# Expert outputs through rows in HBM: scatter by indirect DMA and a token-major final norm

## The reference

```python
def rms_norm(x, g):
    y = x * lax.rsqrt(jnp.mean(x * x, axis=-1, keepdims=True) + EPS)
    return y * g

def moe(h, router, w1, w3, w2):
    logits = h @ router
    top_v, top_i = lax.top_k(logits, TOP_K)
    gates = jax.nn.softmax(top_v, axis=-1)
    dense_gate = jnp.sum(jax.nn.one_hot(top_i, N_EXPERTS) * gates[..., None], axis=-2)
    out = jnp.zeros_like(h)
    for e in range(N_EXPERTS):
        out = out + dense_gate[..., e:e + 1] * swiglu(h, w1[e], w3[e], w2[e])
    return out

x = x + moe(h, ...)
y = rms_norm(x, W['norm_final'])
```

## Time and profile before

| | |
|---|---|
| time, median of 3 runs | 1873.12 us (1873.08 to 1874.67) |
| profiled execution, its own time | 1880.72 us |
| its span, first to last instruction | 1878.6 us |
| PE busy | 1783.1 us, 95% of the span |
| DVE, ACT, POOL busy | 1136.1, 945.4, 81.2 us |
| HBM read and written | 384.78 and 6.08 MB |
| granted TensorE clock, mean | 0.96 of full speed |

### The profile page before, as it was taken

How to read it: one execution, slowest core, us unless ns; L and a number is a source line. 1 busy time by engine, 2 the same in 40 slices (tenths; PEclk the granted TensorE clock), 3 DMA queues, 4 the chain that set the end, 5 groups by cost and what they waited for, 6 DMA issues and landing times.

```text
span 1878.6 us, 32676 instructions
## 1 busy us (share of the span) xinstructions
PE 1783.1 (95%) x13577; PEld 1579.2 (84%) x13577; DVE 1136.1 (60%) x1294; ACT 945.4 (50%) x1073; POOL 81.2 (4%) x136
## 2 busy tenths in 40 slices
PE   7999999999999999999879999999999999999995
PEld 6778878899998788878779889898989989898893
DVE  5166215355543255315348878787887878787884
ACT  2344424353433144333336757676666767665672
POOL 3000110020001000020000000000000000000000
PEclk9999889899999999979879999999999999999998
DMA  8124343155457223435178979898997989899860
GB/s 198 51 91 136 126 123 119 50 173 166 151 154 180 72 86 126 134 102 164 50 264 278 362 262 366 273 365 289 330 366 260 361 274 367 288 332 344 279 214 26
DMA packets 350355, 392.22 MB, mean 209 GB/s; under 512 B 24652, under 2 KB 324840, under 8 KB 350264
## 3 DMA queue, kind: packets, MB, share of 16 engines
q1 hardware_dynamic: 345328, 381.05, 62.1%
q0 software_dynamic: 4640, 9.76, 1.5%
q10 hardware_dynamic: 296, 0.07, 0.0%
HBM read 384.78 MB, written 6.08 MB: 208 GB/s over the span
## 4 chain that ended last, share of the span: by engine, by line
PE 89%; ACT 4%; DVE 4%; issue 1%; DMA 1%; POOL 0%; DVEq 0%; ACTq 0%; SPq 0%
PE ps L607 87%; ACT ring L1106 1%; DVE w_lo L1892 1%; PE ps L1030 1%; ACT w_hi L1106 1%; ACT L1106 1%; ACT kvw_hi L1106 1%; DVE dw_lo L1457 1%; DVE ring L1748 1%; ACT low L1106 0%; DMA ring<-in_ffd_w_dram 0%; PE ps L1080 0%; DMA ring<-in_x_sample_dram 0%; PE ps L905 0%; DVE att L1755 0%
## 5 line engine op out<-in xcount | busy, mean ns | idle before, releaser
L1892 DVE TENSOR_TENSOR w_lo<-ring,w_hi 128x2048 fp32r<-128x2048 f32 x264 | 603.5, 2291 | 86.7 <-ACT w_hi L1106 79.3
L1106 ACT ACTIVATE w_hi<-ring 128x2048 fp32r<-128x2048 f32 x264 | 504.9, 1913 | 139.1 <-PE ps L607 138.4
L607 PE MATMUL ps<-w_hi,hg_hi 128*96 128x256 f32 x1408 | 398.3, 283 | 2.1 <-DVE hg_lo L1869 2.1
L607 PE MATMUL ps<-w_hi,hg_lo 128*96 128x256 f32 x1408 | 394.4, 280 | 0.0
L607 PE MATMUL ps<-w_lo,hg_hi 128*96 128x256 f32 x1408 | 393.8, 280 | 0.0
L607 PEld LDWEIGHTS ps<-w_hi,hg_hi 128*96 128x96 f32 x1408 | 228.1, 162 | 8.7 <-issue 2.3
L607 PEld LDWEIGHTS ps<-w_lo,hg_hi 128*96 128x96 f32 x1408 | 227.4, 162 | 5.7
L607 PEld LDWEIGHTS ps<-w_hi,hg_lo 128*96 128x96 f32 x1408 | 228.6, 162 | 0.0
L1457 DVE TENSOR_TENSOR dw_lo<-ring,dw_hi 128x2048 fp32r<-128x2048 f32 (+1 forms) x54 | 113.1, 2094 | 113.8 <-ACT dw_hi L1106 113.8
L1106 ACT ACTIVATE low<-ps 96x256 f32<-96x256 f32 (+6 forms) x170 | 66.2, 396 | 190.1 <-PE ps L607 179.4
L1106 ACT ACTIVATE dw_hi<-ring 128x2048 fp32r<-128x2048 f32 (+1 forms) x54 | 94.6, 1752 | 101.5 <-PE ps L607 62.1
(11 more groups left out here) (277 smaller groups left out, 2790.6 us busy)
## 6 DMA issues: line engine op xcount, KB each, us to landing
ring<-in_moe_w_dram SPq DMA_DIRECT2D x264, 1024.0 KB, 5.8
ring<-in_ffd_w_dram SPq DMA_DIRECT2D x22, 1024.0 KB, 5.3
ring<-in_ffd_w_dram SPq DMA_DIRECT2D x16, 704.0 KB, 4.6
ring<-in_w_in_dram SPq DMA_DIRECT2D x14, 768.0 KB, 4.5
ring<-in_w_in_dram SPq DMA_DIRECT2D x8, 1024.0 KB, 5.4
ring<-in_xa_wk_dram SPq DMA_DIRECT2D x8, 1024.0 KB, 5.2
ring<-in_xa_wv_dram SPq DMA_DIRECT2D x8, 1024.0 KB, 5.2
ring<-in_xa_wq_dram SPq DMA_DIRECT2D x8, 1024.0 KB, 5.1
```

Of the source, the lines that this page charges most:

```text
L607: return nc.tensor.matmul(out, lhsT, rhs, start=first, stop=last)
L1106: return nc.scalar.activation(out, in_, func, **kw)
L1892: V.tensor_tensor(view(w_lo, off, SLOT), view(ring, moe_slot(u) * SLOT, SLOT), view(w_hi, off, SLOT).bitcast(F32), ALU.subtract).then_inc( ...
```

## The change

The result of an expert no longer goes to `xT` by products on PE. An internal tensor `moe_rows` in HBM has 2 x 288 rows of 1024 numbers, one row for each token's first and second expert, and 96 spare rows. After an expert, DVE copies its unscaled result to `y_sb` (`copy_y`), and POOL writes the 96 rows of it by an indirect DMA to the rows whose numbers stand in `row_at`. POOL waits for that DMA and then signals `y_free`; DVE waits for `y_free` before it writes the next row numbers. The row numbers come from three products in `gather` (`sel` times `id_col`), in the place of the three that gave the gate weights. ACT fills the 576 rows with zeros once, in layer 0, by a DMA from a tile of zeros.

Between the router and the first expert, PE transposes `xT` to token-major form (`turn_x`, 24 transposes) and ACT copies it to `acc`. `small` is transposed, copied and stored there as well. In the last expert, POOL reads the 2 x 288 rows back, and DVE adds them to `acc` with the gate weight of each token as a scalar, three instructions after step 4 and three after step 8 (`add_back`). The last expert's own result is split in high and low part, multiplied by `selT` (12 products of 512 columns) and added to `acc` with its gate weights. The final norm runs token-major: a sum of squares along the row and the root on ACT, one scaling per tile on DVE, and three stores on SP. SP also loads the gains of the final norm, spread over 128 partitions, before it goes on with the ring.

The core of the diff; new semaphores and memory places are left out:

```diff
-            def scatter(n):
-                pe.wait_ge(y_scaled, n + 1)
-                for d in range(KD):
-                    if d >= 4:
-                        pe.wait_ge(scat_added, n * KD + d - 3)
-                    mm(ps[:, 4 + d % 4, 0:T], y_sb[0:C, P * d:P * d + P], selT[0:C, :], True, True).then_inc(scat_ready, 1)
...
                 up(0)
-                scatter(it)
                 up(1)
-                pe.wait_ge(scat_added, it * KD + KD)
-                for t in range(3):
-                    nc.tensor.transpose(ps[0:C, 6, P * t:P * t + P], sel[:, t, :], ident[:, :])
-                for t in range(3):
-                    last = mm(ps[0:C, 6, 384:385], sel[:, t, :], gcol[:, t:t + 1], t == 0, t == 2)
+                if last_one:
+                    for t in range(3):
+                        last = nc.tensor.transpose(ps[0:C, 6, P * t:P * t + P], sel[:, t, :], ident[:, :])
...
+            with pool.Fori(0, more * NE + NE) as it:
+                pool.wait_ge(y_scaled, it + 1)
+                pool.sem_inc(y_taken, 1)
+                pool.indirect_dma_start(rows_y[:, :], bass.IndirectOffsetOnAxis(ap=row_at[0:C, 0:1], axis=0),
+                                        y_sb[0:C, :], None).then_inc(y_put, 16)
+                pool.wait_ge(y_put, it * 16 + 16)
+                pool.sem_inc(y_free, 1)
...
+            gather(1)
+            turn_x(2)
+            b = open_bank("small")
+            close_bank(nc.tensor.transpose(ps[0:32, b, 0:P], small[:, :], ident[:, :]))
+            pe.wait_ge(act_emptied, emptied("xt", 5))
+            pe.wait_ge(small_ready, 1)
...
-            V.memset(ps[0:C, 2:4, :], 0.0)
-            V.memset(gs[0:C, :], 0.0)
-            link(V.memset(selT[0:C, :], 0.0))
...
-                scale_y(it)
+                copy_y(it)
                 weight_lo(it, 2)
-                add_y(it)
                 weight_lo(it, 3)
...
+                    dve.wait_ge(y_free, it + 1)
+                    V.tensor_scalar(row_at[0:C, :], ps[0:C, 6, 0:1], spare_row[0:C, 0:1], None, ALU.add)
...
+                    if last_one and s in (4, 8):
+                        add_back(s // 4 - 1)
...
+            for half in range(2):
+                f(y_hi[0:C, 512 * half:512 * half + 512], ps[0:C, 2 + half, :], ACT.Copy).then_inc(y_hi_done, 1)
+            for t, (t0, rows) in enumerate(TILES):
+                act.wait_ge(acc_ready, t + 1)
+                f(y_sb[0:rows, :], acc[t], ACT.Square, accum_out=msq_y[0:rows, t:t + 1]).then_inc(rs_step, 1)
...
```

More of the change, by code:

```diff
@@ L216, in layer_program @@
         sel = view(low, 6976, 3, C)
-        selT = view(low, 7264, T)
+        tok_no = view(low, 7552, 3, NE)
+        row_no = view(low, 7576, 3, NE)
+        id_col = view(low, 7600, 3)
+        spare_row = view(low, 7604, 1)
+        row_at = view(low, 7606, 1).bitcast(U32)
+        msq_y = view(low, 7608, 3)
+        rs_y = view(low, 7612, 3)
+        ids = view(low, 7616, 3, (MAXR + 1) * NE)
         lgt = view(low, 7936, 3, NE)
@@ L986, in _, with turn_x @@
             close_bank(last)
+            def turn_x(t):
+                t0, rows = TILES[t]
+                for g in range(2):
+                    b_ = open_bank("xt")
+                    for j in range(4):
+                        last_ = nc.tensor.transpose(ps[0:rows, b_, P * j:P * j + P], xT[:, 4 * g + j, t0:t0 + rows],
+                                                    ident[:, :])
+                    close_bank(last_)
+            turn_x(0)
+            turn_x(1)
             pe.wait_ge(rounds_ready, 1)
@@ L1068, in _ @@
             expert(more * NE + (NE - 1), True)
-            scatter(more * NE + NE)
-            pe.wait_ge(scat_added, more * (NE * KD) + (NE + 1) * KD)
-            sum_squares(3 * LAYERS)
-            for t, (t0, rows) in enumerate(TILES):
[L1075 to L1084, removed]
+            pe.wait_ge(selT_ready, 1)
+            for half in range(2):
+                pe.wait_ge(y_hi_done, half + 1)
+                for t, (t0, rows) in enumerate(TILES):
+                    mm(ps[0:rows, (0, 4, 6)[t] + half, :], selT[0:C, t0:t0 + rows], y_hi[0:C, 512 * half:512 * half + 512],
+                       True, False)
+            for t, (t0, rows) in enumerate(TILES):
+                for half in range(2):
+                    pe.wait_ge(y_lo_done, half + 1)
+                    last = mm(ps[0:rows, (0, 4, 6)[t] + half, :], selT[0:C, t0:t0 + rows],
+                              y_lo[0:C, 512 * half:512 * half + 512], False, True)
+                last.then_inc(scat_ready, 1)
         @block.scalar
@@ L1418, in expert, with x_copy @@
                         weight_hi(it + 1, u)
-            for u in range(SPLITS):
+            def x_copy(t):
+                rows = TILES[t][1]
+                for g in range(2):
+                    b_ = take("xt")
+                    if t == 2:
+                        act.wait_ge(chunk_ready, CHUNK_NO["xt", 5] + 1)
+                    f(acc[t][:, 512 * g:512 * g + 512], ps[0:rows, b_, :], ACT.Copy).then_inc(act_emptied, 1)
+            weight_hi(0, 0)
+            x_copy(0)
+            x_copy(1)
+            for u in range(1, SPLITS):
                 weight_hi(0, u)
@@ L1938, in expert, with add_back @@
                         weight_lo(it + 1, u)
+            def add_back(i):
+                dve.wait_ge(y_back, 32 * (i + 1))
+                for t, (t0, rows) in enumerate(TILES):
+                    if i:
+                        dve.wait_ge(y1_added, 1)
+                    ins = V.scalar_tensor_tensor(out=acc[t], in0=y_in[0:rows, t, :], scalar=cols[0:rows, 9 - 3 * i + t:10 - 3 * i + t],
+                                                 in1=acc[t], op0=ALU.mult, op1=ALU.add)
+                if i == 0:
+                    ins.then_inc(y1_added, 1)
+                else:
+                    link(ins)
+            for r in range(MAXR + 1):
+                V.tensor_tensor(ids[:, :, NE * r:NE * r + NE], row_no[:, :, :], posr[:, :, NE * r:NE * r + NE], ALU.subtract)
             weight_lo(0, 0)
             weight_lo(0, 1)
+            b = take("small")
+            V.tensor_copy(stage3[0:32, :], ps[0:32, b, 0:P]).then_inc(small_ready, 1)
             gather_lo(1)
+            dve.wait_ge(act_emptied, emptied("xt", 5))
             with dve.Fori(0, more * NE + (NE - 1)) as it:
```

134 lines of the change are left out of this document (95 added, 39 removed).

## The result

The changed kernel takes 1818.66 us (median of four runs, 1817.36 to 1819.59) beside 1873.89 us for the kernel before on the same chip (1873.08 to 1878.51). The ratio is 0.9687, 95% interval 0.9665 to 0.9708. A second set gave 1817.75 us and 0.9674 (0.9644 to 0.9704). That is faster than the range of 1822 to 1846 us: the prediction had the direction and most of the mechanism, and missed 13 us of gain. In three later sets the median of before was 1879.32, 1876.27 and 1876.30 us, so the 1873.12 us that the prediction started from lay low.

The account below looks back on a forecast made before the run. PE was taken as the bound, with DVE and the DMA queues next. Terms of -32.3 - 2.7 + 4.0 - 11.4 + 0 + 1.0 = -41.4 us took the median from 1873.1 to 1831.7 us; range 1822 to 1846 us.

Parts of the forecast that it names:

- the tail: From the last product to the last store's landing: gain 11.4 us, bounds 8 and 13.
- The clock term: Long gathers, five of seven, might become none or seven at 1.63 us each: 0 taken, bounds -8.2 and +3.3.
- Ahead of the experts: Earlier, possibly shorter first gather against added products, transposes and copies before the first up: 0 taken, bounds -2.5 and +1.5.
- Zeros and the stretch ahead: Layer 0: ACT's 2.36 MB of zero writes delay weights PE waits for, +1 us, bounds 0 and 6.
- scatter: PE's products adding an expert's result to xT: eight inside experts at 4.04 us go, 32.3 us gained.
- transposes and gate products: In the experts, transposes and gate products leave PE, row-number products come: 2.7 us net gain.
- no price for the weights: At an expert's start PE still gets w_lo and a_lo in time: nothing charged, margins 0.2 to 0.3 us.
- no price for `y_free`: DVE's new wait for the indirect DMA: 7 us taken, 10.7 us available, so nothing charged.
- the two stops of `add_back`: Last expert: two groups of three DVE additions stop PE 2.0 us each, +4.0 us, bounds 0 and 7.7.
- DMA not the bound: In the experts the queues keep up at 337 GB/s; the rival, DMA bound at 1866 us, had 0.07.
- the one of more gained by the clock: Rival: the upper clock level is kept in the gathers as well, time below 1823 us; chance 0.07.
- POOL's reading beside `w_lo`: POOL's row-number read might wait out a w_lo, 2.29 us, making the landing 9.3 us; left out of the 7 us.

Follow-up runs that it names:

- e5: Kernel before with only the small states' transpose, copy and POOL's four stores moved ahead of the experts: 1868.54 us, ratio 0.9950.
- e1: Changed kernel with a_hi and a_lo of step 9 made ahead of unit 32's w_hi and w_lo at an expert's end: 1801.71 us, ratio 0.9577.
- e2: Kernel before with a_hi and a_lo of step 9 made ahead of unit 32's w_hi and w_lo: 1848.09 us, ratio 0.9832.
- e6: Changed kernel with PE's 16 transposes of xT for two tiles moved behind the first gather: 1833.32 us, one execution.
- e4: Changed kernel with eight DVE reductions, results unused, in place of the scatter's eight additions in seven experts: 1836.44 us, ratio 0.9782.
- e10: Changed kernel run once more, unedited: 1817.75 us, ratio 0.9674.
- e3: Changed kernel with the eight scatter products put back on PE in seven experts, results not added: 1861.77 us, ratio 0.9919.
- e8: Changed kernel with e1's reordering and the last expert's six additions spread one per step: 1799.83 us, ratio 0.9567.
- e7: Changed kernel with each indirect DMA issued a second time after the first landed, y_free after both: 1883.01 us, one execution.
- e9: Changed kernel with six of the eight scatter products put back on PE in seven experts, results not added: 1864.64 us, ratio 0.9940.

## Why the prediction missed, step by step

The error is 21 us against the profiled executions, of which the translation to the median takes 7.6 off (before's profiled execution stood that far above its first three runs; after's stands 0.8 below its median).

*The step that failed first: the tail*, 11.4 us with bounds 8 and 13, measured 20.9. "Now" was off by 2.2 us, the landing: 2.0 us for 4.2. The larger part is "before": the sum ended at the last landing on the page, 1871.3, while the span ended at 1878.6. Those 7.3 us had no term, and I let them stand in both kernels. They are POOL's closing DRAIN, 7.0 us from 1871.4 on, behind its four late stores; the trace of the kernel before has the row, and the prediction did not use it. e5 shows that this is what ended the kernel: with the stores early the DRAIN is early too, and the span ends at the landing of SP's last store. The landing that the page gives was right and was not the end. Why the DRAIN takes 7.0 us here and 14.0 in the changed kernel, no run shows.

*The clock term*, "0 taken, since the wait ahead of the gather stays as it is", measured 6.5 us. The wait did stay, 2.0 us. That it then gives five long gathers was read from one profile. e1 and e2 show that the wait is what makes them (no wait, none long). The counts of 1, 3, 5 and 5 in the changed kernel, e6, e4 and before, with the same wait, show that it only makes them possible. What decides between long and short stays open. The Trainium skill (TensorE: Matmul & The Clock Gate, Part 1: The HAM clock gate (the "warmup" mystery)) says that the monitor of PE's activity runs free and is not reset by a kernel's start. The different counts would fit that, but no run shows the monitor, and e10, whose long gather was the same one again, does not speak for it. The saving had been within the stated bounds of -8.2 and +3.3; that the count fell and did not rise was not forecast, and the middle of the bounds, a gain of 2.4, would have been fairer than 0.

*Ahead of the experts*, 0 taken, bounds -2.5 and +1.5, measured -2.75. The lower bound named the cause and nearly the size, and I took the middle. e6 shows the cause: PE, busy through the wait, kept 2.4 GHz.

*Zeros and the stretch ahead*: +1 taken, -1.4 measured. The end of the rank products moves by 11 us between profiles of kernels that are alike up to there, so no run here gives the zeros a price.

*Right:* scatter (4.04 by e3), transposes and gate products (an expert with a short gather falls from 106.96 to 102.65 us, 4.31 for 4.37), no price for the weights (margin 0.2 us by e4), no price for `y_free` (7.9 us for 7), the two stops of `add_back` (3.5 by e8 for 4.0), the 10.4 us to the last scaling, and DMA not the bound. Of the rivals, the one of more gained by the clock, given 0.07, came in its number and only in part in its cause: the clock gave 6.5 us, but without the 9.5 us that the tail was off the time would have been some 1828 us, inside the range.

*POOL's reading beside `w_lo`.* The prediction left this wait out of its 7 us, by rows of other instructions, and priced it at a whole `w_lo`, 9.3 us in all. It is there, and smaller: POOL's indirect DMA ends 0.77 to 0.85 us after the `w_lo` during which it began, whatever its own length. The changed kernel's first one, where less of the `w_lo` was left (DVE, then POOL), beside the rows 1602.50 and 1603.38 above:

```profile
983.09 2.28 DVE L1973 TENSOR_TENSOR w_lo<-ring,w_hi 128x2048 fp32r<-128x2048 f32 x1
984.50 1.72 POOL L643 DMA_INDIRECT moe_rows<-low  x1 [1.17 <-issue]
```

It lasts 1.72 us with 0.87 us of the `w_lo` left, 2.17 us with 1.40 left, and up to 2.66 us with 1.89 left (e7's second DMAs). POOL's plain DMAs, which read no list of rows (L650, L652), took 0.52 to 0.78 us and ended while a `w_lo` still ran. So at most 1.4 of the 7.9 us are this wait, and the time to spare covered it. The rule of the Trainium skill (SBUF — State Buffer, Who interferes with whom) that the prediction cites says that a DVE instruction with two SBUF inputs contends with a GpSimd instruction that reads SBUF; the trace agrees.

## What to carry to other kernels

A pause on the engine that bounds costs its length and, at times, the lower clock behind it; count how many pauses of that kind a profile has, and give the clock an expected value between its bounds, not the value that keeps things as they are. Compare the span's end with the last landing that the page shows: a gap there belongs to someone, and the rows of the engines' closing instructions say to whom. Let the engine with a long closing instruction finish its work early. Look at the bounding engine's waits for a producer queued behind work that isn't needed yet: moving one instruction ahead of another, on ACT and on DVE, gave 19 to 26 us between the cuts here.

## What I had not expected of the hardware

- A loop on PE that grew by six products and a wait stands still at each turn for 2.0 to 3.0 us, six times, and the instruction queue moves 125 packets for 71 (e3, e9). The Trainium skill (Runtime: NRT & Kernel Launch, Instruction fetch mechanics) says that a taken branch to code no longer at hand forces a load by DMA before the engine goes on; the nine packets more at each turn agree.
- A stop of 5.8 us on PE cost another 2.15 us in the step behind it (e7, granted clock 0.50 from 1228.1 to 1232).
- A stop of 2.0 us ahead of a gather cost nothing more, 1.63 us more or 3.0 to 3.2 us more (e6, e9), in gathers that are alike.
- POOL's closing DRAIN takes 7.0 us in the kernel before and in e5, and 14.0 in the changed kernel. Behind four stores of 16 KB in all, issued last, it kept the kernel 7.3 us beyond their landing.
- An indirect DMA on POOL that begins during a DVE instruction with two SBUF inputs ends 0.77 to 0.85 us after it (all eight in the changed kernel, all sixteen in e7).
- At 35.0 MB an expert the queues moved 341 GB/s at a share of 1.00, and 348 GB/s at 1.02 in e1, and no engine waited for a load: a full share is not yet a bound.
